# Two-layer decoder trunk: experts of the first sweep without a loop, and layer norms whose variance is taken on ScalarE

## What is computed

```python
x = layer_norm(ALPHA * x + deltanet_mixer(x), g[0,0], b[0,0])       # norm(0)
x = layer_norm(ALPHA * x + dense_swiglu(x),   g[0,1], b[0,1])       # norm(1)
x = layer_norm(ALPHA * x + sliding_window_attention(x), g[1,0], b[1,0])   # norm(2)
x = layer_norm(ALPHA * x + moe_swiglu(x),     g[1,1], b[1,1])       # norm(3)

def layer_norm(x, g, b):
    mu = mean(x); xc = x - mu; var = mean(xc * xc)
    return xc * rsqrt(var + 1e-5) * g + b

def moe_swiglu(x):       # 8 experts, top 2 of a token, weights 1024 x 5632 and 2816 x 1024 each
    out = 0
    for e in range(8):
        h = x @ w_gu[e]
        out += gates[:, e] * ((silu(h[:, :2816]) * h[:, 2816:]) @ w_down[e])
```

## Time and profile before

| | |
|---|---|
| median of three runs | 1341.6 us (1340.52 to 1343.66) |
| the profiled execution | 1341.11 us, of which 1339.4 us are the span of the trace |
| TensorE matmul busy | 1262.7 us (94%) |
| VectorE busy | 996.3 us (74%) |
| ScalarE busy | 819.4 us (61%) |
| GpSimd busy | 92.1 us (7%) |
| granted TensorE clock, mean | 0.98 of full speed |

### The profile page before, as it was taken

One profiled execution on the slowest core, in us unless ns is written; L12 is line 12 of the kernel. 1 busy time (PEld: TensorE's weight loads), 2 busy tenths in 40 slices (PEclk: granted clock), 3 DMA queues, 4 the chain that ended last, 5 costly groups with the idle time before them and its releaser, 6 DMA issues.

```text
span 1339.4 us, 19224 instructions
## 1 busy us (share of the span) xinstructions
PE 1262.7 (94%) x7097; PEld 1097.1 (82%) x7097; DVE 996.3 (74%) x824; ACT 819.4 (61%) x798; POOL 92.1 (7%) x112
## 2 busy tenths in 40 slices
PE   6999998999999979999999999999999999999990
PEld 5997996999988967888888788887888888888880
DVE  4876844545546575688888788897898888888883
ACT  4885343344433364477777777776777777778760
POOL 3034201200001100200000000000000000000002
PEclk9999998999999999999999999999999999999995
DMA  9734001897554512599999999999999999999963
GB/s 315 225 126 157 2 32 63 317 374 240 178 194 146 189 64 94 209 383 405 389 387 359 376 365 378 388 384 354 359 371 382 385 386 355 381 404 373 383 229 111
DMA packets 188730, 375.48 MB, mean 280 GB/s; under 512 B 12224, under 2 KB 69680, under 8 KB 188624
## 3 DMA queue, kind: packets, MB, share of 16 engines
q1 hardware_dynamic: 179744, 345.02, 71.5%
q0 software_dynamic: 6576, 24.76, 5.0%
q10 hardware_dynamic: 2304, 4.31, 0.8%
HBM read 354.12 MB, written 19.92 MB: 279 GB/s over the span
## 4 chain that ended last, share of the span: by engine, by line
PE 87%; DVE 6%; ACT 3%; issue 2%; POOL 1%; DMA 1%; POOLq 0%; SPq 0%; DVEq 0%; ACTq 0%
PE ps L1257 84%; PE ps L1641 1%; POOL lnrs L381 1%; DVE lo L828 1%; DVE conv L888 1%; DVE bnst L851 1%; DVE x L861 1%; ACT hi L516 1%; DVE x L847 1%; ACT sS L698 1%; PE ps L1634 0%; DMA picked<-ys,row 0%; DMA x<-in_x 0%; DVE x L1249 0%; PE ps L1268 0%
## 5 line engine op out<-in xcount | busy, mean ns | idle before, releaser
L828 DVE TENSOR_TENSOR lo<-raw,hi 128x2048 fp32r<-128x2048 f32 x327 | 747.0, 2297 | 188.0 <-ACT hi L516 187.0
L516 ACT ACTIVATE hi<-raw 128x2048 fp32r<-128x2048 f32 x327 | 627.1, 1919 | 349.4 <-PE ps L1257 332.0
L1257 PE MATMUL ps<-hi,xg_hi 128*128 128x512 f32 x704 | 279.2, 397 | 6.3 <-issue 6.3
L1257 PE MATMUL ps<-hi,xg_lo 128*128 128x512 f32 x704 | 276.0, 392 | 0.0
L1257 PE MATMUL ps<-lo,xg_hi 128*128 128x512 f32 x704 | 275.4, 391 | 0.0
L1257 PE MATMUL ps<-xT_hi,hi 128*128 128x256 f32 x624 | 177.5, 284 | 2.1 <-DVE xT_lo L836 2.1
L1257 PE MATMUL ps<-xT_hi,lo 128*128 128x256 f32 x624 | 176.6, 283 | 0.0
L1257 PE MATMUL ps<-xT_lo,hi 128*128 128x256 f32 x624 | 176.6, 283 | 0.0
L1257 PEld LDWEIGHTS ps<-hi,xg_hi 128*128 128x128 f32 x704 | 133.0, 189 | 35.3 <-issue 7.4
L1257 PEld LDWEIGHTS ps<-hi,xg_lo 128*128 128x128 f32 x704 | 132.8, 189 | 28.4
L1257 PEld LDWEIGHTS ps<-lo,xg_hi 128*128 128x128 f32 x704 | 133.2, 189 | 26.7
(11 more groups left out here) (264 smaller groups left out, 1264.5 us busy)
## 6 DMA issues: line engine op xcount, KB each, us to landing
raw<-in_moe_w_gu SPq DMA_DIRECT2D x352, 512.0 KB, 7.4
raw<-in_moe_w_down SPq DMA_DIRECT2D x176, 512.0 KB, 6.5
raw<-in_ffn_w_gu SPq DMA_DIRECT2D x44, 512.0 KB, 8.0
raw<-in_dn_w_in SPq DMA_DIRECT2D x32, 512.0 KB, 8.1
raw<-in_ffn_w_down SPq DMA_DIRECT2D x22, 512.0 KB, 4.2
xe<-xTf POOLq DMA_DIRECT2D x1, 8192.0 KB, 29.1
raw<-in_dn_w_out SPq DMA_DIRECT2D x8, 512.0 KB, 3.8
ys<-xTf POOLq DMA_DIRECT2D x1, 4096.0 KB, 40.6
```

Of the source, the lines that this page charges most:

```text
L516: act.activation(slot(hi, j), slot(raw, j), ACT.Copy).then_inc(hi_ready, 1)
L828: dve.tensor_tensor(slot(lo, j), slot(raw, j), slot(hi, j).bitcast(F32), ALU.subtract).then_inc(lo_ready, 1)
L1257: return pe.matmul(dst, lhsT, rhs, start=start, stop=stop)
```

## The change

Three things are changed. The short way of working out the route stays as it is.

1. In the first sweep (`p` is 0) the four turns are written out on SP, PE, ACT and DVE. The second sweep keeps its loops.
2. The norm's mean and variance. DVE's add gives the row's sum as well (`accum_out`); two small multiplies make -mean/32 and mean. ACT (`deviation`) computes Square(x/32 - mean/32) over the row with its sum, written to unused PSUM banks, which is the variance, and adds 1e-5. Centring writes to PSUM, and the last operation reads from there. In norm(3) the second weighted sum gives the row's sum, and block 1's sums come before block 0's last operation.
3. ACT's order around the norms: each block's `deviation` stands between the cuttings of the last units, ahead of the copies of the transposed blocks, and one cutting is moved behind those copies.

```diff
-            def experts(base):
-                with sp_.Fori(0, TURNS) as it:
-                    for l in range(PER_IT):
-                        expert_unit(base, l, it)
+            def experts(p):
+                base = U_MOE + p * E * PER_E
+                if p:
+                    with sp_.Fori(0, TURNS) as it:
+                        for l in range(PER_IT):
+                            expert_unit(base, l, it)
+                else:
+                    for it in range(TURNS):
+                        for l in range(PER_IT):
+                            expert_unit(base, l, it)
...
+            def deviation(i, b, bank):
+                act.wait_ge(ln_mean, 2 * i + b + 1)
+                act.activation(ps[:, bank + 2 * b:bank + 2 * b + 2, :].rearrange("p b n -> p (b n)"), x[:, b, :], ACT.Square,
+                               scale=1.0 / 32, bias=lnmu32[:, b:b + 1], accum_out=lnvr[:, b:b + 1]).then_inc(ln_square, 1)
+                act.wait_ge(ln_square, 2 * i + b + 1)
+                act.activation(lnve[:, b:b + 1], lnvr[:, b:b + 1], ACT.Copy, bias=1e-5).then_inc(ln_var, 1)
...
-            for u in range(4):
-                cut_hi(U_OUT + u + AHEAD)
+            cut_hi(U_OUT + 0 + AHEAD)
+            cut_hi(U_OUT + 1 + AHEAD)
+            deviation(0, 0, 4)
+            cut_hi(U_OUT + 2 + AHEAD)
+            deviation(0, 1, 4)
             turn(2)
+            cut_hi(U_OUT + 3 + AHEAD)
...
-            for u in range(FC):
+            for u in range(FC - 2):
                 cut_hi(U_DOWN + u + AHEAD)
+            deviation(1, 0, 0)
+            cut_hi(U_DOWN + FC - 2 + AHEAD)
+            deviation(1, 1, 0)
             turn(3)
+            cut_hi(U_DOWN + FC - 1 + AHEAD)
...
-            for u in range(1, 4):
-                cut_hi(U_O + u + AHEAD)
+            cut_hi(U_O + 1 + AHEAD)
+            deviation(2, 0, 4)
+            cut_hi(U_O + 2 + AHEAD)
+            deviation(2, 1, 4)
...
             for i in range(3):
                 xT_copy(i)
+            cut_hi(U_O + 3 + AHEAD)
...
-                with act.Fori(0, TURNS - 1) as it:
-                    turn_of(it, False)
+                if p:
+                    with act.Fori(0, TURNS - 1) as it:
+                        turn_of(it, False)
+                else:
+                    for it in range(TURNS - 1):
+                        turn_of(it, False)
                 turn_of(TURNS - 1, True)
...
+            for b in range(NB):
+                deviation(3, b, 4)
...
             def norm(i, bank, last=None):
...
+                def mean(b):
                     if bank is not None:
...
+                        step(dve.scalar_tensor_tensor(out=x[:, b, :], in0=x[:, b, :], scalar=ALPHA, in1=pair(bank, b),
+                                                      op0=ALU.mult, op1=ALU.add, accum_out=lnsum[:, b:b + 1]))
+                    else:
+                        dve.wait_ge(picked_here[b], 32)
+                        step(dve.scalar_tensor_tensor(out=x[:, b, :], in0=picked[:, b, 0, :], scalar=gw[:, b, 2:3],
+                                                      in1=x[:, b, :], op0=ALU.mult, op1=ALU.add))
+                        step(dve.scalar_tensor_tensor(out=x[:, b, :], in0=picked[:, b, 1, :], scalar=gw[:, b, 3:4],
+                                                      in1=x[:, b, :], op0=ALU.mult, op1=ALU.add, accum_out=lnsum[:, b:b + 1]))
+                    dve.tensor_scalar(lnmu32[:, b:b + 1], lnsum[:, b:b + 1], -1.0 / (32 * D), None, ALU.mult).then_inc(ln_mean, 1)
+                    step(dve.tensor_scalar(lnmu[:, b:b + 1], lnsum[:, b:b + 1], 1.0 / D, None, ALU.mult))
+
+                def centre(b):
                     if b == 0:
                         dve.wait_ge(ln_here, 32 * (i + 1))
-
-                    step(dve.scalar_tensor_tensor(out=x[:, b, :], in0=x[:, b, :], scalar=bnmv[:, b, 0:1], in1=lng[:, :],
+                    link(dve.scalar_tensor_tensor(out=pair(bank or 0, b), in0=x[:, b, :], scalar=lnmu[:, b:b + 1], in1=lng[:, :],
                                                   op0=ALU.subtract, op1=ALU.mult))
+
+                def finish(b):
+                    settle()
                     dve.wait_ge(ln_rstd, 2 * i + b + 1)
-                    dve.scalar_tensor_tensor(out=x[:, b, :], in0=x[:, b, :], scalar=lnrs[:, b:b + 1], in1=lnb[:, :],
+                    dve.scalar_tensor_tensor(out=x[:, b, :], in0=pair(bank or 0, b), scalar=lnrs[:, b:b + 1], in1=lnb[:, :],
                                              op0=ALU.mult, op1=ALU.add).then_inc(ln_done[b], 1)
+
+                mean(0)
+                centre(0)
+                if bank is None:
+                    mean(1)
+                    finish(0)
+                else:
+                    finish(0)
+                    mean(1)
+                centre(1)
+                finish(1)
```

More of the change, by code:

```diff
@@ L93, in trunk @@
         mhalf = sb("mhalf", [P, NB * H])
-        bnst = sb("bnst", [P, NB, 2, 6])
-        bnmv = sb("bnmv", [P, NB, 2])
+        lnvr = sb("lnvr", [P, NB])
+        lnsum = sb("lnsum", [P, NB])
+        lnmu = sb("lnmu", [P, NB])
+        lnmu32 = sb("lnmu32", [P, NB])
         lnve = sb("lnve", [P, NB])
@@ L199, in trunk @@
         turned, turn_hi, turn_lo = sem("turned"), sem("turn_hi"), sem("turn_lo")
-        ln_var, ln_rstd, ln_done = sem("ln_var"), sem("ln_rstd"), [sem(f"ln_done{b}") for b in range(NB)]
+        ln_mean, ln_square, ln_var, ln_rstd, ln_done = sem("ln_mean"), sem("ln_square"), sem("ln_var"), sem("ln_rstd"), [sem(f"ln_done{b}") for b in range(NB)]
         conv_step, tap_ready, silu_done = sem("conv_step"), sem("tap_ready"), sem("silu_done")
@@ L310, in expert_unit @@
                     load(base + l, it, mdown_v[u - GU_E][e], "p (k n) -> p k n", k=2)
-            def experts(base):
-                with sp_.Fori(0, TURNS) as it:
-                    for l in range(PER_IT):
-                        expert_unit(base, l, it)
-            experts(U_MOE)
+            def experts(p):
[8 more added lines that the diff above has]
+                            expert_unit(base, l, it)
+            experts(0)
             sp_.wait_ge(route_here, 1)
@@ L320, in _ @@
             with sp_.If(full > P):
-                experts(U_MOE + E * PER_E)
+                experts(1)
             for b in range(NB):
@@ L839, in norm, with pair @@
             def norm(i, bank, last=None):
-                for b in range(NB):
+                def pair(bank, b):
+                    return ps[:, bank + 2 * b:bank + 2 * b + 2, :].rearrange("p b n -> p (b n)")
+                def mean(b):
                     if bank is not None:
@@ L846, in norm @@
                             used(last)
[L847 to L852, removed]
@@ L853, in norm @@
-                    step(dve.bn_aggr(bnmv[:, b, :], bnst[:, b, :, :].rearrange("p q s -> p (q s)")))
-                    dve.tensor_scalar(lnve[:, b:b + 1], bnmv[:, b, 1:2], 1e-5, None, ALU.add).then_inc(ln_var, 1)
+                        step(dve.scalar_tensor_tensor(out=x[:, b, :], in0=x[:, b, :], scalar=ALPHA, in1=pair(bank, b),
[6 more added lines that the diff above has]
+                                                      in1=x[:, b, :], op0=ALU.mult, op1=ALU.add, accum_out=lnsum[:, b:b + 1]))
@@ L1236, in experts @@
                     route()
-                with dve.Fori(0, TURNS - 1) as it:
-                    turn_of(it, False)
+                if p:
+                    with dve.Fori(0, TURNS - 1) as it:
+                        turn_of(it, False)
+                else:
+                    for it in range(TURNS - 1):
+                        turn_of(it, False)
                 turn_of(TURNS - 1, True)
@@ L1245, in _ @@
             dve.wait_ge(x_scaled, 1)
[L1246 to L1250, removed]
             norm(3, None)
@@ L1689, in experts @@
                     turn_xg(E * p)
-                with pe.Fori(0, TURNS - 1) as it:
-                    turn_of(it, False)
+                if p:
+                    with pe.Fori(0, TURNS - 1) as it:
+                        turn_of(it, False)
+                else:
+                    for it in range(TURNS - 1):
+                        turn_of(it, False)
                 turn_of(TURNS - 1, True)
```

## The result

The changed kernel takes 1324.63 us (median of 4 runs, 1323.0 to 1327.18), the kernel before 1341.06 in the same comparison (4 runs, 1338.86 to 1343.66). The ratio is 0.9878, 95% interval 0.9854 to 0.9903. It is faster, by 16.4 us, where 11.7 were forecast and 1327.6 was the low end of the range. The profiled execution takes 1325.1 us, with a span of 1323.0 and a mean granted clock of 0.98.

A forecast was written before the change was run, and what follows sets the result against it. TensorE holds 87% of the chain that ended last, so time is won where it stalls, slows or is off the chain. -9.6 - 3.0 + 0.9 = -11.7 us on 1341.1, median 0.5 higher: 1329.9 us, range 1327.6 to 1333.4.

The forecast's parts named there:

- The written-out sweep: Experts' first sweep: without loop jumps TensorE loses its stalls and the low clock behind them, 9.6 us less.
- They are not on the path there: Jumps of ACT, DVE and SP in the experts' sweep: off the path, so their gain was not counted.
- Norms one to three: First three layer norms: the new mean and variance cost 0.03 us more a block, taken as 0.
- 1.92 against 1.83: nothing gained: Norms one to three, from the add's end to GpSimd's start: new steps 1.92 us, old ones 1.83.
- The third norm: ScalarE's copies wait for the second block's mean and Square, delaying the logits: +0.9 us, bounds -0.5 and +1.5.
- if it falls earlier, the logits get slower: Norm three: the low clock may come earlier and slow the logits; within the upper bound of +1.5 us.
- The last norm: Tail: block one's chain overlaps block two's weighted sums, -3.0 us, bounds -2.2 and -3.4.
- A sum at half rate: Rival: DVE operations giving a sum run at half rate with two SBUF inputs; tail 2.6 us more, 1332.5; chance 0.12.
- ScalarE's detour: Rival: variance through ScalarE takes 0.35 us per block longer than the statistics, +2.5, 1332.4 us; chance 0.08.
- The weights kept up: Rival, experts' sweep: weights do not keep up, half of the 9.6 us returns as DMA waits, 1334.7; chance 0.05.
- Code written out: Rival: written-out code is fetched as it goes, over memory that the weights fill; 1352 us at 0.5 each; chance 0.03.
- The stall was the jump's: Rival claimed the opposite: the stall is not the jump's, only the tail is won, 1339.5 us; chance 0.04.

The follow-up runs named there:

- u2: The kernel before with only TensorE's three looped turns written out, the other engines keeping their loops: 1333.86 us (one run).
- u3: The kernel before with SP, ACT and DVE written out and TensorE's loop kept: 1336.85 us (one run).
- p2: The kernel before with the add's result of the first three norms left in PSUM, so the centring reads one SBUF input: 1340.18 us, ratio 0.9992.
- p3: The changed kernel with each centring issued twice, so one with two SBUF inputs runs when the power starts: 1325.69 us (one run).
- c1: The changed kernel with ScalarE's first two copies of transposes ahead of the second Square in norm three: 1320.2 us, ratio 0.9845 to the kernel before.
- u1: The kernel before with the first sweep written out on all four engines and nothing else: 1333.16 us, ratio 0.9945.
- u6: The kernel before with TensorE and ScalarE written out, VectorE and SyncE in their loops: 1333.31 us (one run).
- u5: The kernel before with TensorE looping over single experts (six jumps back) and the other three engines written out: 1331.84 us (one run).
- n1: The changed kernel with the loops of before put back, so the new norms alone: 1335.54 us, ratio 0.9970 to the kernel before.

## Why the prediction was wrong

The direction and the largest term were right; the size fell short by 4.7 us, and 1324.63 lies 3 us below the range. By the profiled executions the 4.7 are made up of 2.9 in norms one and two, 3.0 in stages in which nothing was changed, 0.9 in the sweep and 0.3 in the tail, less 2.4 in norm three. The error in norm three runs the other way and hid most of that in norms one and two. Step by step:

- **The written-out sweep, right in kind, 0.9 too small.** The stalls were the jumps', and the low clock behind them went with them. The step that made turn four, with its eight transposes put back, a measure of 187.02 us was 0.35 too long: a turn takes 186.67. The fourth is shorter by 0.53 us and not by 0.88. It is counted to the last matmul's full end, 0.16 past where a next one would start, and the others only to the next one's start; that is half of the 0.35, the other half stays open. The three turns come out 0.15, 0.35 and 0.35 shorter than counted.
- **"They are not on the path there" of the other engines' jumps was wrong.** No idle time of TensorE showed it. But with TensorE alone written out (u2) ScalarE's loop costs 3.6 us, and with TensorE's loop kept (u3) the others' loops cost 4.1. The total was not hurt, since all went: the forecast had put the whole stall and slow stretch down to TensorE's jump. Of the 10.5 us that the sweep gained, 6.4 to 6.9 are TensorE's, the rest the other engines'. So 9.6 came out near for a reason that is in part another than the one given.
- **Norms one to three, the step that failed.** The term "1.92 against 1.83: nothing gained" was right for what stands between add and power: 3.00 us from add to power against 3.05. The error was to take GpSimd's 1.53 as the power's own price. It was the rest of the centring and 0.40 more, as p2 and p3 show; the power alone is 0.55. The new order lets the centring end before the power starts (229.00 against 229.20). It saves 1.02 us in a block. Block two's add gets only 0.44 of it, for it then waits for TensorE; so a norm saves 1.44, and norms one and two 2.9.
- **The third norm, right in kind, too small.** Forecast +0.9, bounds -0.5 and +1.5; the stage took +3.3 between these two executions, although norm three's blocks are shorter too. ScalarE's order did what was said: the copies waited for the second Square, and the second block's transposes stood behind TensorE's own fill. But the bounds left out that TensorE's 1.78 us of waiting would be followed by some 10 us at the low clock; I had considered "if it falls earlier, the logits get slower" and given it 0.6 us at most. Part of the +3.3 is which executions were compared, for the length of the slow stretch varies with either order.
- **The last norm, right.** -3.30 against -3.0. The order made the overlap that was described, with both powers held (1.42 and 1.45).
- **Not forecast:** 1.5 us in attention, 0.6 ahead of norm one and 0.9 in the gather. Nothing was changed in these stages. Ahead of norm one kernels with the same code there took 224.4 to 226.8, and attention with norm two took 100.1 us in the changed kernel and 102.9 in c1, which has the same order there; its low clock (0.83 for one window of 10 us against 0.56 and 0.93 in two) moves. That is spread between executions, and I can't say what sets it.
- **The rivals.** A sum at half rate did not occur: the operation takes 1.29 us with two SBUF inputs against 1.28 without a sum. That speaks against the rule of the Trainium skill, Vector Engine (DVE) Microarchitecture Reference, section Points that are easy to get wrong, which the prediction cites for this form. ScalarE's detour was not longer than counted. The weights kept up. Code written out brought no idle time and fewer packets. The stall was the jump's, or rather, the long body's.

## What to carry to other kernels

Before an instruction's duration is taken as its price, look at what runs beside it: a GpSimd operation under a running VectorE instruction with two SBUF inputs shows the other's remaining time, and here the order of the two was worth 1 us a block where it was on the path. A loop's price is not in its number of jumps but in whether its body is kept, and in what the loop's head loads again; the next engine's loop appears once the first is gone. Where TensorE's feed is reordered, price the idle time with the slow stretch behind it: here an order that made TensorE wait 1.4 to 1.8 us cost 2.8 to 5.8.

## What the runs showed of the hardware

- The read of a sum on VectorE is a record of its own of 0.08 us, and the next instruction starts 0.12 us after it does.
- In its loop ScalarE loads a function table twice each time round, at the head (1.28 us, with 1.0 to 1.3 ahead of it behind a jump) and 5 to 10 us later at line 774 (1.28 us). Written out, the four turns have one such load in all (u1, u6 and the changed kernel).
- A jump back costs TensorE 0.03 us where the body is kept (u5). Where a body of 136 KB is not, TensorE stands still for 3.04 to 3.24 us with all engines in loops (before, n1, p2), and for 2.43 and 1.56 us when the others are written out (u3).
- The last operation of a block takes 1.28 us with one input in PSUM and one in SBUF, while the add takes 1.22 with the same kinds of inputs. The 0.06 us a block that I had counted back didn't come.
